# A GELU's three elementwise steps moved from VectorE to GpSimd in a hybrid decoder trunk

## The reference

```python
z = h @ w_in
c_q, c_kv, k_r, x_rec, g_rec = jnp.split(z, IN_SPLITS, axis=-1)
...
attn = _causal_attention(qf, kf, v, positions)
xr = _causal_conv(x_rec, conv_w, conv_b)
rec = _rglru(xr, w_a, b_a, w_x, b_x, lam) * jax.nn.gelu(g_rec)
y = jnp.concatenate([_rms(attn, ...), _rms(rec, ...)], axis=-1)
return y @ w_out
```

## Time and profile before

| | us |
|---|---|
| median of 3 runs | 1624.14 |
| lowest and highest | 1623.41, 1626.88 |
| the profiled execution | 1621.45 |
| its span | 1619.7 |
| granted clock of TensorE, mean share of full | 0.962 |
| VectorE busy | 1254.2 |
| ScalarE busy | 902.0 |
| GpSimd busy | 13.2 |

### The profile page before, as it was taken

The page is one execution under the profiler, slowest core; times in us unless marked ns, Lnnn a source line. Parts: engine busy times, 40 slices in busy tenths (PEclk is TensorE's granted clock), DMA queues, the critical chain, the costliest instruction groups (busy, mean ns, idle before and its releaser), DMA issues.

```text
span 1619.7 us, 19746 instructions
## 1 busy us (share of the span) xinstructions
PE 1487.6 (92%) x7629; PEld 1244.8 (77%) x7629; DVE 1254.2 (77%) x1067; ACT 902.0 (56%) x786; POOL 13.2 (1%) x53
## 2 busy tenths in 40 slices
PE   4977699997577869999999999999999999999998
PEld 1756699997456758887887887887887887887886
DVE  3476477673467169989989989998998998998998
ACT  2170443432036037766766766776776776776775
POOL 1000000000000000000000000000000000000000
PEclk8998799998798979999999999999999999999999
DMA  9930949850961158999989989989989999998990
GB/s 356 353 130 1 337 156 353 293 208 1 367 263 54 70 191 312 375 334 333 380 332 342 371 331 344 373 325 351 370 322 352 369 354 333 360 379 321 346 378 32
DMA packets 190958, 467.68 MB, mean 289 GB/s; under 512 B 8423, under 2 KB 31173, under 8 KB 186821
## 3 DMA queue, kind: packets, MB, share of 16 engines
q1 hardware_dynamic: 186464, 450.12, 75.8%
q0 software_dynamic: 2224, 16.78, 2.6%
q10 hardware_dynamic: 2228, 0.22, 0.1%
HBM read 466.04 MB, written 1.05 MB: 288 GB/s over the span
## 4 chain that ended last, share of the span: by engine, by line
PE 80%; DVE 8%; ACT 5%; DMA 3%; issue 3%; DVEq 1%; SPq 0%; ACTq 0%; POOL 0%; POOLq 0%
PE ps L872 17%; PE ps L870 17%; PE ps L871 17%; PE ps L751 4%; PE ps L753 4%; PE ps L752 4%; PE ps L734 4%; DMA arena<-in_w_ada 3%; PE ps L831 2%; PE ps L850 2%; DVE split_r L1684 2%; PE ps L907 2%; PE ps L592 1%; PE ps L541 1%; PE ps L585 1%
## 5 line engine op out<-in xcount | busy, mean ns | idle before, releaser
L1684 DVE TENSOR_TENSOR split_r<-arena,split_r 128x2048 fp32r<-128x2048 f32 x339 | 770.8, 2289 | 69.9 <-ACT split_r L1161 69.0
L1161 ACT ACTIVATE split_r<-arena 128x2048 fp32r<-128x2048 f32 x339 | 649.5, 1916 | 151.7 <-PE ps L872 151.7
L870 PE MATMUL ps<-split_r,tokens_r 128*128 128x512 f32 x1280 | 511.0, 399 | 0.7 <-DVE tokens_r L1691 0.7
L872 PE MATMUL ps<-split_r,tokens_r 128*128 128x512 f32 x1280 | 499.2, 390 | 0.0
L871 PE MATMUL ps<-split_r,tokens_r 128*128 128x512 f32 x1280 | 498.3, 389 | 0.0
L870 PEld LDWEIGHTS ps<-split_r,tokens_r 128*128 128x128 f32 x1280 | 240.4, 188 | 52.5 <-issue 4.8
L871 PEld LDWEIGHTS ps<-split_r,tokens_r 128*128 128x128 f32 x1280 | 240.6, 188 | 51.4 <-issue 3.8
L872 PEld LDWEIGHTS ps<-split_r,tokens_r 128*128 128x128 f32 x1280 | 240.2, 188 | 51.0
L751 PE MATMUL ps<-tokens_r,split_r 128*128 128x256 f32 x528 | 150.5, 285 | 4.5 <-DVE hT_r L1566 4.5
L753 PE MATMUL ps<-tokens_r,split_r 128*128 128x256 f32 x528 | 150.2, 284 | 0.0
L751 PEld LDWEIGHTS ps<-tokens_r,split_r 128*128 128x128 f32 x528 | 102.3, 194 | 4.9 <-issue 4.9
(11 more groups left out here) (313 smaller groups left out, 1389.6 us busy)
## 6 DMA issues: line engine op xcount, KB each, us to landing
arena<-in_moe_w_gate SPq DMA_DIRECT2D x57, 2048.0 KB, 8.7
arena<-in_moe_w_up SPq DMA_DIRECT2D x57, 2048.0 KB, 8.2
arena<-in_moe_w_down SPq DMA_DIRECT2D x56, 2048.0 KB, 8.3
arena<-in_w_ada SPq DMA_DIRECT2D x15, 1024.0 KB, 7.4
arena<-in_w_ada POOLq DMA_DIRECT2D x10, 1536.0 KB, 10.7
arena<-in_ffn_w_gate SPq DMA_DIRECT2D x11, 1024.0 KB, 6.4
arena<-in_ffn_w_up SPq DMA_DIRECT2D x11, 1024.0 KB, 9.3
arena<-in_ffn_w_down SPq DMA_DIRECT2D x11, 1024.0 KB, 13.6
```

The source lines that it names most:

```text
L870: mm(out_, xh, h, start=first, stop=False, skip_group_check=True)
L872: return mm(out_, xl, h, start=False, stop=last_, skip_group_check=True)
L1161: A(wh[:, j % SPLITS, :], piece_half(j), ACT.Copy).then_inc(sem("w_hi"), 1)
L1684: v.tensor_tensor(wl[:, j % SPLITS, :], piece_half(j), wh[:, j % SPLITS, :].bitcast(F32), ALU.subtract).then_inc(sem("w_lo"), 1)
```

## The change

In each layer GpSimd takes the polynomial, its product with g and the last product. GpSimd's last product has no added one, so ScalarE adds it in a pass of its own after the tanh, and signals `g_tanh` twice in a layer. VectorE gets a wait for `lq_free` ahead of L1513.

```diff
@@ GpSimd, each layer, after it has signalled wbd_zero
+                pool.wait_ge(sem("g_sq"), l + 1)
+                g.tensor_scalar(lq, lq, GELU_A, 1.0, ALU.mult, ALU.add).then_inc(sem("g_poly"), 1)
+                pool.wait_ge(sem("g_poly"), l + 1)
+                g.tensor_tensor(lq, lq, gr, ALU.mult).then_inc(sem("g_arg"), 1)
+                pool.wait_ge(sem("g_tanh"), 2 * l + 2)
+                g.tensor_tensor(gr, lq, gr, ALU.mult).then_inc(sem("lq_free"), 1)
                 if l == 0:
                     for kind, a, k, cell, waits in late:
@@ ScalarE
                 act.wait_ge(sem("g_arg"), l + 1)
                 A(lq, lq, ACT.Tanh, scale=GELU_B).then_inc(sem("g_tanh"), 1)
+                act.wait_ge(sem("g_tanh"), 2 * l + 1)
+                A(lq, lq, ACT.Copy, bias=1.0).then_inc(sem("g_tanh"), 1)
                 turned_q(1, 6)
@@ VectorE
                 heads(0)
-                dve.wait_ge(sem("g_sq"), l + 1)
-                link(v.tensor_scalar(lq, lq, GELU_A, 1.0, ALU.mult, ALU.add))
-                v.tensor_tensor(lq, lq, gr, ALU.mult).then_inc(sem("g_arg"), 1)
                 heads(1)
...
-                dve.wait_ge(sem("g_tanh"), l + 1)
-                v.scalar_tensor_tensor(out=gr, in0=lq, scalar=1.0, in1=gr, op0=ALU.add, op1=ALU.mult)\
-                    .then_inc(sem("lq_free"), 1)
                 row_max(1, 6, 2, SEQ, 0)
...
                 link(last)
+                dve.wait_ge(sem("lq_free"), l + 1)
                 v.scalar_tensor_tensor(out=lx, in0=lq, scalar=-0.5, in1=gr, op0=ALU.mult, op1=ALU.mult)\
                     .then_inc(sem("rec"), 1)
```

## The result

The changed kernel takes 1635.62 us (median of 4 runs, 1633.30 to 1636.10) against 1625.20 us for the kernel before, run beside it (4 runs): a ratio of 1.0061, with a 95% interval from 1.0044 to 1.0079. That is 10.4 us slower, where I had forecast slower by 6.6, and 1.6 us above the upper end of the range. (Of the 4.9 us between 1635.62 and the forecast of 1630.7, 1.1 is the kernel before, whose median was 1624.14 where I started from it and 1625.20 beside the changed kernel; 3.8 is the forecast's own.)

A forecast was written before the change was run, and what follows sets the result against it. The prediction took a closed chain of waits through each layer's mixer as the bound; per layer 2.8 + 0.65 - 0.15 = 3.3 us, two layers 6.6, so 1624.14 + 6.6 = 1630.7 us, range 1622.8 to 1634.

The forecast's parts named there:

- VectorE's standing: In the last taps and rotary steps, VectorE stands while GpSimd reads SBUF: 2.8 us per layer, range 0 to 3.5.
- one in which it gets in among them: GpSimd's product starts among the last taps, so VectorE stands another 2.25 us after the polynomial's 1.25: together 3.5.
- TensorE's clock: Ahead of the first transposes a longer wait likely lowers the clock: 0.65 us per layer, bounds 0 and 1.3.
- The likeliest case: GpSimd blocks VectorE among the taps: 4.4 to 9.3 us slower in all, 1628.5 to 1633.5; blocking as forecast or worse, 0.50.
- GpSimd's prices: GpSimd's polynomial was taken at 1.25 us (0.95 to 1.5), a product at 2.25 (0.95 to 2.7).
- The 0.15 us of the second transposes: At the second L644, heads(1) ending earlier lets the weight load overlap better: 0.15 us gained per layer, between 0 and 0.38.
- The 1.21 us of L1488: Taking this step off VectorE only widens its idle time ahead of row maximum L1475: gain 0.
- ScalarE's pass: Adding the one after the tanh takes 1.06 us but ends before the turned queries: price 0, or 0.35 without VectorE's lead.
- No meeting: VectorE and GpSimd don't hinder each other in taps and rotary steps: -0.3 us in all, 1623.8; chance 0.27.
- the kind order: GpSimd waits for the taps, its product under one-input instructions: 1 us per layer, no clock fall, 1625.8; chance 0.14.
- GpSimd the bound: GpSimd's two steps take over 13 us and delay the tanh; at 3 us each, blocking, about 1636; chance 0.04.
- the freed VectorE: Steps outside the chain would have to yield 3.2 us, only by a changed clock phase: 1620.6; chance 0.05.

The follow-up runs named there:

- before_reads: The kernel before plus two GpSimd instructions reading SBUF after the square, like the polynomial and product, on unneeded tiles: 1637.10 us, ratio 1.0076.
- late_start: The changed kernel with GpSimd held back until VectorE's rotary sums of heads(1), about 92 us in layer 0: 1627.34 us, ratio 1.0013.
- after_busy_pe: The changed kernel with TensorE's last pair of up-projection matmuls of each mixer done three times over: 1629.92 us, ratio 1.0034.
- the second profile: The changed kernel, without further edits, profiled once more in one run: 1634.36 us.
- start_in_heads0: The changed kernel with GpSimd held back only until VectorE's rotary sums of heads(0), about 86.6 us: 1630.35 us, ratio 1.0035.
- before_filled: The kernel before with dummy TensorE transposes after the attention products in both layers and ahead of layer 0's output projection: 1624.52 us, ratio 0.9994.

## Why the prediction was right and where it was wrong

**The place was right.** The chain runs through the last taps, GpSimd's reads hold it up there, in both layers, and all of it reaches the end. `before_reads` and `late_start` show that from both sides: the reads without the change cost as much as the change, and the change without the meeting in the taps costs the mixers nothing.

**VectorE's standing: the size right, the order not.** I took 2.8 us per layer; it is 2.75. That these agree is in part luck. For I took the order in which the product waits for the taps to end, and held it against one in which it gets in among them, for 3.5. It did get in among them: the polynomial holds one tap, the product the next for 2.57 us, and L1398 starts straight after the taps. The 3.5 was too much because VectorE does not stand for all of GpSimd's time: the polynomial starts 0.3 us before the last four taps, and the tap that it held runs on between it and the product.

**TensorE's clock: the step that failed.** It read "I count half, 0.65 for each layer, with bounds 0 and 1.3". Held against the 7.33 us of `after_busy_pe`, where the clock stays up, the distance between the groups of transposes is 3.30 and 3.47 us longer in the first profile and 1.11 and 3.36 in the second: 2.8 on average, and over the bound of 1.3 in three layers of four. That it falls was foreseen; how long it stays low was not. I priced one group of transposes at 1.3 and then took half of it. In layer 0 of the first profile, from the first transposes to the scores of the first tokens, it cost 1.57 us (4.85 against 3.28), near that price; the scores themselves, at the low clock until about 102 us, cost another 1.72 (4.05 against 2.33), for which I had no term. `gates(0)`, at 102.75, had the high clock again. In layer 0 of the second profile the clock was back by 98 us, for the scores, and the price was 1.1. `after_busy_pe` shows that it is the clock: with TensorE kept at work, 5.7 us of the 10.4 are gone. In the terms of the prediction the sum per layer is 2.75 + 2.8 - 0.15 = 5.4, or 10.8 in all, in place of 6.6. The likeliest case reached up to 9.3 and so fell short of the 10.4 measured; its lower end, 2 x 2.2, stands there without a working.

**GpSimd's prices**, bounded from the earlier trace rows, were near: 1.05 us for the polynomial undisturbed against 1.25, and 2.35 for the products against 2.25. The tanh did not wait for `g_arg`, nor the square root for `lq_free`: in the changed kernel the product is done at 87.11 and the tanh starts at 99.98.

**The gains.** The 0.15 us of the second transposes measured 0.15 in `after_busy_pe` (7.33 against 7.48) and 0.10 in `late_start`. The 1.21 us of L1488 went into VectorE's wait ahead of the row maximum, which grew from 1.26 to 2.38 us. ScalarE's pass cost 0 in the changed kernel and about 0.2 us ahead of `turned_q` in `late_start`, where VectorE's lead is gone, used up by the three small steps that stand in `heads(1)` (0.35 was the prediction's price for that).

**The rivals.** No meeting (0.27) and the kind order (0.14) didn't come about. `start_in_heads0` was built as the kind order and shows that there is a further victim in it: the small steps L1458. My 1 us for that order rested on the product fitting under the sums of squares; in `start_in_heads0` the standing is 1.76 us and the clock falls as well. Nor was GpSimd the bound, with 1.20 and 2.40 us for its two steps. And the freed VectorE paid nothing.

**Open.** `late_start` is 0.5 to 3.6 us over before, by its interval, and its mixers are no longer than before's. Its profiled execution, 1624.41 us, is 2.9 below its median and so may not hold the loss. What lies behind the mixers has the same instructions and varied by 4.5 us between two profiles of the same kernel. What the 2 us are the runs don't tell.

## What to carry to other kernels

Before work goes to an idle GpSimd, look at what VectorE does on the chain in that very stretch: an instruction of GpSimd that reads SBUF stops VectorE's instructions with two SBUF inputs, and some with one, for nearly its whole length. The same work 9 us later cost the chain nothing here, not because it met nothing but because VectorE had 1.9 us in hand and lost 1.8. Price a wait on the chain together with the clock of the engine that waits, and price everything that will run at the low clock, not only the first group: 0.8 us per layer left TensorE's clock alone, 2.0 made it fall and cost more than itself. And where VectorE's freed time only lengthens its waits, there is nothing to gain that would pay for the risk.

## What the runs showed of the hardware

- VectorE's 128x256 taps with both inputs in SBUF took 0.48 us alone, up to 1.26 us beside a GpSimd `tensor_scalar` and up to 2.57 us beside a `tensor_tensor`, and twelve of them 5.09 us with and without GpSimd memsets beside them. Reductions from SBUF beside GpSimd's polynomial kept their 0.69, 0.41 and 0.68 us. Three one-input steps of 8 columns took 2.26 us (`start_in_heads0`) and 2.27 (`late_start`) beside its product in place of 0.50.
- GpSimd took 1.05 us for a `tensor_scalar` and 2.35 us for a `tensor_tensor` of 128x1024 in float32, and 1.20 and 2.40 where they met the taps in layer 0 (2.51 for the `tensor_tensor` alone).
- TensorE's granted clock fell to 0.50 in a wait of 4 us and was still there 8 us after TensorE had gone back to work (94 to 102 us); in the second profile of the same kernel it was back after 4 us in layer 0. With the wait cut to 0.6 us by dummy matmuls it stayed at 1.00; in layer 1 of `before_filled` it fell after 4.54 us of dummy matmuls and 1.93 us of waiting.
- The same kernel, unchanged, had the clock at 1.00 in one profile and at 0.50 in another from 112 to 118 us of layer 0.
